# Two chunks of a triangular inversion run five steps ahead of the other two, and a masking step is issued one step later

## What is computed

```
m = where(strict, einsum(k_beta, k) * decay, 0)
t_inv = triangular_solve(eye + m, eye)
u = t_inv @ (v * beta);  w = t_inv @ (k_beta * exp(g))
for each chunk:                                   # the scan
    v_new = u_i - w_i @ state
    o = (q_i * exp(g_i)) @ state + a_i @ v_new
    state = state * exp(g_last) + k_dec^T @ v_new
```

## Time and profile before

| what | us |
|---|---|
| median of 3 runs | 1057.03 (1056.55 to 1057.26) |
| the profiled execution, its own time | 1057.9 |
| its span in the trace | 1056.1 |
| stretch from the last projection to the first x step | 186.64 to 235.66 |
| stretch of the levels, x7 and t | 235.66 to 349.72 |
| from there to the scan's second kb product | 349.72 to 364.26 |

### The profile page before, as it was taken

How to read it: one execution, slowest core, us unless ns; L and a number is a source line. 1 busy time by engine, 2 the same in 40 slices (tenths; PEclk the granted TensorE clock), 3 DMA queues, 4 the chain that set the end, 5 groups by cost and what they waited for, 6 DMA issues and landing times.

```text
span 1056.1 us, 12807 instructions
## 1 busy us (share of the span) xinstructions
PE 972.5 (92%) x5186; PEld 820.8 (78%) x5186; DVE 499.6 (47%) x812; ACT 470.4 (45%) x821; POOL 450.8 (43%) x253
## 2 busy tenths in 40 slices
PE   6999798759999899999998979899999999999987
PEld 5987576649999797777776758788888888888876
DVE  5057764487675345324246432433333333564434
ACT  6464566435654144334376541453333433332223
POOL 4528344570002363143577642245354443454440
PEclk9999999869999899999999999999999999999998
DMA  9423110000001007133322222133323232333302
GB/s 352 133 77 98 62 41 1 1 1 1 2 27 55 1 22 259 52 120 100 89 72 61 64 86 71 47 114 100 100 83 117 80 107 93 100 100 100 100 20 80
DMA packets 25162, 84.07 MB, mean 80 GB/s; under 512 B 2992, under 2 KB 3248, under 8 KB 24976
## 3 DMA queue, kind: packets, MB, share of 16 engines
q1 hardware_dynamic: 24240, 82.14, 23.9%
q10 hardware_dynamic: 864, 1.12, 0.3%
HBM read 79.06 MB, written 2.10 MB: 77 GB/s over the span
## 4 chain that ended last, share of the span: by engine, by line
PE 74%; DVE 12%; ACT 8%; POOL 3%; issue 2%; DMA 0%; SPq 0%; DVEq 0%; ACTq 0%
PE bank L1889 72%; DVE qk L1439 2%; PE bank L1897 2%; ACT wh L1111 1%; ACT L1111 1%; POOL wl L1005 1%; DVE xl L1433 1%; DVE dd L1433 1%; DVE vc L1439 1%; ACT sl L1111 1%; DVE mp L1433 1%; ACT ee L1111 1%; ACT xs L1111 1%; ACT qk L1111 1%; DVE xf L1433 1%
## 5 line engine op out<-in xcount | busy, mean ns | idle before, releaser
L1005 POOL TENSOR_TENSOR wl<-raw,wh 128x1024 fp32r<-128x1024 f32 (+1 forms) x131 | 316.6, 2421 | 389.8 <-ACT wh L1111 389.7
L1889 PE MATMUL bank<-xh,wh 128*128 128x512 f32 (+1 forms) x536 | 207.8, 388 | 6.8 <-DVE xl L1433 4.8
L1889 PE MATMUL bank<-xh,wl 128*128 128x512 f32 (+1 forms) x536 | 205.9, 384 | 0.0
L1889 PE MATMUL bank<-xl,wh 128*128 128x512 f32 (+1 forms) x536 | 205.9, 384 | 0.0
L1111 ACT ACTIVATE wh<-raw 128x1024 fp32r<-128x1024 f32 (+1 forms) x131 | 135.7, 1042 | 133.5 <-PE bank L1889 127.3
L1889 PE MATMUL bank<-wh,xh 128*128 128x512 f32 (+1 forms) x352 | 140.1, 398 | 18.1 <-POOL wl L1005 10.4
L1889 PE MATMUL bank<-wh,xl 128*128 128x512 f32 (+1 forms) x352 | 135.0, 384 | 0.0
L1889 PE MATMUL bank<-wl,xh 128*128 128x512 f32 (+1 forms) x352 | 134.8, 383 | 0.0
L1889 PEld LDWEIGHTS bank<-xh,wh 128*128 128x128 f32 x536 | 101.5, 189 | 28.2 <-issue 6.0
L1889 PEld LDWEIGHTS bank<-xh,wl 128*128 128x128 f32 x536 | 101.4, 189 | 19.8
L1889 PEld LDWEIGHTS bank<-xl,wh 128*128 128x128 f32 x536 | 101.5, 189 | 19.0
(11 more groups left out here) (249 smaller groups left out, 1566.4 us busy)
## 6 DMA issues: line engine op xcount, KB each, us to landing
raw<-in_wflat SPq DMA_DIRECT2D x127, 512.0 KB, 3.4
xt<-in_xt SPq DMA_DIRECT2D x8, 256.0 KB, 4.3
h<-in_x SPq DMA_DIRECT2D x4, 512.0 KB, 6.8
h<-in_x SPq DMA_DIRECT2D x1, 2048.0 KB, 9.7
gain<-in_pr SPq DMA_DIRECT2D x3, 512.0 KB, 3.4
consts<-in_cf SPq DMA_DIRECT2D x1, 1472.0 KB, 10.8
raw<-in_wflat SPq DMA_DIRECT2D x4, 272.0 KB, 10.9
kh<-kh SPq DMA_DIRECT2D x8, 128.0 KB, 2.3
```

The costliest lines, as they stand in the source:

```text
L1005: e.tensor_tensor(WL[u % NS][:, 0:n], RAW[u % NS][:, 0:n], WH[u % NS][:, 0:n].bitcast(F32), ALU.subtract).then_inc(w_lo.up(u), 1)
L1889: return e.matmul(o, l, r_, start=start, stop=stop, skip_group_check=part)
```

## The change

Three things change.
- DVE's masking of mp into dd and ACT's copy of mp into mr leave the step m. They become a step of their own, inv_dd, which stands at the head of the next step of the same chunk, ahead of mt.
- The order: chunks 0 and 3 are taken through decay, kq, m and mt first, with seven steps of attention between. Then come 14 rounds: one step of chunk 0, two of attention, one of chunk 3, two of attention, and then one step of chunk 1, one of attention, one of chunk 2, one of attention. Chunks 1 and 2 begin these rounds with their decay, so they are five steps behind. After the 14 rounds, chunks 0 and 3 are done and chunks 1 and 2 have five steps left (d at level 5, x and d at level 6, x7, t).
- The first vb of the scan waits for the inverse of chunks 0 and 3.

```diff
--- before.py
+++ after.py
@@ -515,6 +515,7 @@
         BI.let_go(("inv", cb, "k"))
         do("inv_m", cb)
         yield
+        do("inv_dd", cb)
         for d in range(2):
             take(("mt", d), (inv_v, ("dt", cb, 0, d)))
         do("inv_mt", cb)
@@ -600,19 +601,25 @@
             step(gi[0])
     while step(g1):
         pass
-    step(gi[1], 2)
     BI.over((0, 1, 2, 3, 4))
     gs = swa()
     for b in (5, 6, 7):
         BANK[("swa", b)] = (b, emptied[b])
-    for g in gi[2:]:
-        step(g, 2)
+    for cb, n in ((0, 1), (3, 2), (0, 1), (3, 1), (0, 1), (3, 1), (3, 1)):
+        step(gi[(0, 3, 1, 2).index(cb)], n)
+        step(gs)
+    ahead = 14
     live = True
-    while live:
+    while ahead or live:
         live = False
-        for g in gi:
+        for g in gi[:2]:
+            if ahead:
+                step(g)
+                step(gs, 2)
+        ahead -= ahead > 0
+        for g in gi[2:]:
             live = step(g) or live
-            step(gs, 2)
+            step(gs, 1 if ahead else 2)
     do("z_gain")
     while step(gs):
         pass
@@ -1060,7 +1067,7 @@
             W = SCAN[d]
             if r == 0:
                 on.wait_ge(*inv_v.at(("t", 0, 1)))
-                on.wait_ge(*inv_v.at(("t", 2, 1)))
+                on.wait_ge(*inv_v.at(("t", 3, 1)))
                 on.wait_ge(*swa_g.at(3))
             else:
                 on.wait_ge(*scan_p.at(("av", d, r - 1)))
@@ -1256,7 +1263,7 @@
             on.wait_ge(*inv_a.at(("ee1", cb, d)))
             act(ee, ee, ACT.Exp, inv_a.up(("ee", cb, d)), scale=-1.0)
 
-        def inv_m(cb):
+        def inv_mr(cb):
             for d in range(2):
                 on.wait_ge(*inv_g.at(("m", cb, d)))
                 act(WORK[cb]["MR"][d][:], MP[cb][:, d, :], ACT.Copy, inv_a.up(("mr", cb, d)))
@@ -1418,7 +1425,7 @@
             e.dma_start(ov[:, tb, 0:512], OUT[:, tb, 0:512]).then_inc(s_out[0], 16)
 
         return dict(begin=begin, x_split=x_split, rms_row=rms_row, prep=prep, stat=stat, split=split, conv=conv, square=square, qsum=qsum, qexp=qexp, to_tok=to_tok,
-                    gate1=gate1, gate2=gate2, rope_root=rope_root, rope_t=rope_t, tok=tok, inv_decay=inv_decay, inv_m=inv_m,
+                    gate1=gate1, gate2=gate2, rope_root=rope_root, rope_t=rope_t, tok=tok, inv_decay=inv_decay, inv_dd=inv_mr,
                     inv_d=inv_d, swa_s=swa_s, swa_t=swa_t, swa_o=swa_o, scan_keys=scan_keys, scan_v=scan_vn, scan_o=scan_o,
                     dn_sq=dn_sq, forget=forget, cum_a=cum_a, gelu=gelu, qk2=qk2, fa_exp=fa_exp, fa_t=fa_t, fa_o=fa_o_, fa_split=fa_split,
                     gm_root=gm_root, up_post=up_post,
@@ -1601,6 +1608,9 @@
             for d in range(2):
                 on.wait_ge(*inv_g.at(("mb", cb, d)))
                 tt(MP[cb][:, d, :], psum[b][:, :], W["MB"][d][:], ALU.mult, inv_v.up(("m0", cb, d)))
+
+        def inv_dd(cb):
+            W = WORK[cb]
             for d in range(2):
                 on.wait_ge(*inv_g.at(("m", cb, d)))
                 tt(h3(W["DD"][d][:]), h3(MP[cb][:, d, :]), bc4(cf("LM", 7 * (1 - d))), ALU.mult, inv_v.up(("dd", cb, 0, d)))
@@ -1874,7 +1884,7 @@
                 stt(OUT[:, tb, c], H[:, tb, c], rr, GAIN[:, c], ALU.mult, ALU.mult, fin_v.up(("out", tb, n)))
 
         return dict(begin=begin, x_split=x_split, conv_rms=conv_rms, scale=scale, split=split, masks=masks, conv=conv, qexp=qexp, gate1=gate1, gate2=gate2, rope_sq=rope_sq,
-                    rope_root=rope_root, rope_scale=rope_scale, rope=rope, rope_t=rope_t, inv_decay=inv_decay, inv_kq=inv_kq, inv_m=inv_m,
+                    rope_root=rope_root, rope_scale=rope_scale, rope=rope, rope_t=rope_t, inv_decay=inv_decay, inv_kq=inv_kq, inv_m=inv_m, inv_dd=inv_dd,
                     inv_mt=inv_mt, inv_x=inv_x, inv_d=inv_d, inv_x7=inv_x7, inv_t=inv_t, swa_s=swa_s, swa_t=swa_t, swa_o=swa_o,
                     scan_o=scan_o, dn_mul=dn_mul, tok=tok, resid=resid_, fa_const=fa_const, forget=forget, cum_b=cum_b, qk2=qk2, fa_s=fa_s,
                     fa_norm=fa_norm, fa_t=fa_t, fa_o=fa_o_, fa_split=fa_split, gm_sum=gm_sum, gm_rec=gm_rec, gm_norm=gm_norm, gm=gm, up_post=up_post, a_prep=a_prep,
```

## The result

The changed kernel is slower: 1100.07 us (median of 4 runs, 1094.29 to 1100.66) against 1057.14 of the kernel before. The ratio is 1.0381, with a 95% interval of 1.0357 to 1.0404. The forecast was 1047.0, with a range of 1041 to 1055.

A forecast was written before the change was run, and what follows sets the result against it. PE issue bounds the levels; 35 us are lost in the masking stretch and handover, with DVE the next bound. Gains 5.9 - 1.5 + 5.6 = 10.0 us take 1057.9 to 1047.9 profiled, 1047.0 median; range 1041.0 to 1055.0.

The forecast's parts named there:

- The stretch of levels: Rounds behind the masking (x and d steps): PE's work unchanged and still the bound, 1.7 us lost before.
- Rival D: Masking stretch: clock stays low as PE is thinly fed, 362 instructions take 82.5 us, kernel ends at 1067.0; chance 0.07.
- Edit 1: dd and mr one step later: DVE's four direct waits for POOL go (3.1 us), dd kept at 1.34 us.
- rival C: Masking stretch: dd no longer meets POOL, costs 0.68 instead of 1.34, 5.3 us off; time 1041.7; chance 0.15.
- Edit 2's first stretch: Chunks 0 and 3 ahead, until all masking is done: DVE-bound, 62.5 us, 21.2 lost against 27.1, gain 5.9 us.
- The tail of two chunks: Inversion's end with chunks 1 and 2: they do not quite cover the last division, loss 1.5 us (0 to 3).
- Edit 3: Handover to the scan: first vb waits for chunks 0 and 3; 8.9 us where 14.5 stood, gain 5.6 us.
- Rival B: Handover gains nothing: attention's end, z_gain and vb come too late, PE waits for vb; time 1052.6; chance 0.10.
- Rival A: Masking stretch gains nothing: DVE idle 14.4 us again, chain through POOL is the bound; time 1052.9; chance 0.12.
- The sum: Whole kernel: 5.9 - 1.5 + 5.6 = 10.0 us gained, profiled execution 1047.9, median 1047.0 us.

The follow-up runs named there:

- Experiment 1: Changed kernel plus 12 PE filler products of 512 columns before chunk 0's d step at level 3; 1047.47 us, ratio 0.9886.
- experiment 6: Changed kernel plus wide PE fillers before chunk 0's d steps at level 2 (10) and level 3 (12); 1048.20 us, ratio 0.9902.
- experiment 9: Changed kernel plus 24 narrow PE fillers of 128 columns before chunk 0's d step at level 3; 1048.30 us, ratio 0.9894.
- experiment 5: Kernel before plus six extra DVE multiplies ahead of chunk 0's xf at level 2, to make PE wait; 1125.98 us, ratio 1.0625.
- experiment 4: Kernel before, old order and old scan wait, with only dd and mr moved one step later; 1136.63 us, ratio 1.0726.
- experiment 2: Changed kernel plus 12 wide PE fillers before chunk 0's d step at level 5; median 1078.66 us, profiled run 1059.4.
- experiment 3: Changed kernel with dd and mr put back in the step m, so without their delay; 1057.59 us, ratio 0.9989.
- experiment 10: Kernel before with dd one step later, plus 16 wide PE fillers before chunk 0's d step at level 1; 1064.64 us, ratio 1.0061.
- experiment 12: Changed kernel plus 24 narrow PE fillers of 128 columns before chunk 0's d step at level 5; 1103.49 us, ratio 1.0433.
- experiment 7: Changed kernel plus 12 wide PE fillers at chunk 0's level 3 and 14 before mt of chunks 0 and 3; 1052.11 us, ratio 0.9946.

## Why the prediction was wrong, point by point

**The stretch of levels** is the step that failed. The prediction wrote: "The work of PE is the same and stays the bound", and gave it a loss of 1.7 us for small waits and 1.5 for the division. It priced a wait of PE by its own length. Two waits of 2.4 us together stand where the clock fell, and 51.4 us more go by behind them, because every instruction costs 0.213 us instead of 0.114 until chunk 0's x7. Experiments 1, 6, 9 and 5 show it from both sides: with products in the place of the first wait the new order takes 1047.5 to 1048.3, and the old order with such waits takes 1126.0. What in the work behind a wait lifts the clock, and what leaves it down, stays open.

**Rival D** had the right mechanism, a clock that stays low, and was given 0.07. Its place and its size were wrong. It was put into the thin rounds up to round 5, where the clock was at 0.50 from 200 to 215 us and then came back (0.86 over the first of the windows above), and was bounded by that stretch's 362 instructions. I took the dense stretch to be safe because in the earlier trace rows it ran at 1.00. But those rows show only that it keeps the clock it comes with, not that it would take it back.

**Edit 1** was read as harmless. The prediction let DVE's direct waits (3.1 us) go and kept dd at 1.34 us. In the new order 2.5 us of the waits stay, 1.74 for chunk 0 and 0.78 for chunk 3: with one step of attention between, POOL's addition isn't done. Only the old order loses them (0.0 in experiment 4). The prediction did not ask what stands around the new place: dt behind, the attention maximum behind that, and POOL's at masks beside. dd came to 1.48 us in the new order and 1.56 in the old one, rival C's 0.68 is what the shortest takes and no mean is near it, and by itself the edit costs 78 us (experiment 4).

**Edit 2's first stretch** had the right bound, and DVE's work came out: 51.9 us against 51.5. The rest did not: the sum put 11 us on it (9 of idle DVE, 2 of slow clock), and DVE was idle for 13.8. The stretch took 65.7 us against 62.5. At 0.114 each its 373 instructions are worth 42.5 us, and PE was busy for 50.9, so that slow clock cost PE 8.4 us there. What the sum had as 21.2 us of loss was 23.2, and the gain 3.9 us instead of 5.9. A stretch that DVE bounds has PE waits somewhere; the prediction summed them and did not say where each would fall. Where they fall decided the case.

**The tail of two chunks** was right in kind and too dear: PE waited 0.40 us for the xf behind the last division, where the sum has a loss of 1.5:

```profile
385.25 1.17 PE L1899 MATMUL bank<-xf,dd 128*128 128x128 f32 x8 [0.40 <-DVE xf L1440]
```

**Edit 3** was right: 9.15 us against 8.9, by the bank and not by vb. Rival B is out. Rival A is out by its time but not by its sign: DVE was idle for 13.8 us, near its 14.4. Its price was wrong: by the prediction's own terms 51.5 and 14.4 make 65.9 us, nearly what was measured, and that is a gain of 2.5 us and not of nothing.

**The sum** of all but the clock came out, and in part by luck. Experiment 1's profiled execution took 1047.3 us, and the forecast for one was 1047.9. But its first stretch took 65.7 us and not 62.5. The work behind it up to PE's last t took 92.3, where the sum has 96.2 (816 instructions at 0.114, 1.7 and 1.5). The two errors cancel. The gain of the change, with a filler in it, is some 10 us, and the clock's price about five times that.

On the clock the Trainium skill (TensorE: Matmul & The Clock Gate, Part 1) says that the throttled state is the default and that activity releases it. For the first half the traces show only that the clock is at 0.50 behind waits. The second does not cover these traces: PE was busy for 110.8 of 110.8 us in the changed kernel, 140 of 140 in experiment 5 and 189.3 of 190 in experiment 4, and the clock was not released. Here the measurement decides.

## What to carry to other kernels

Where long runs of small products follow a place at which PE may wait, price the wait by the clock behind it and not by its length, and look in the trace for what last raised the clock and whether it still comes after the new wait. A step moved behind another one is to be looked at with its new neighbours on its own queue and on GpSimd's, not only freed of its old wait. If a schedule that should win comes out slower at a low granted clock, a few spare products in the wait are a cheap test, and here they were also the better kernel (1047.5 us against 1058.1).

## What was not expected of the hardware

- PE was busy for 189.3 of 190 us and stayed at 1.2 GHz (experiment 4). Between 186 us and the end of the inversion the clock came back in or right behind kq products (202 us before), in the products of the decay steps (216 us in the changed kernel), in mt transposes (230 us before, about 258 us in experiments 2 and 3), in x7 steps (363 us in the changed kernel, about 406 us in experiment 5), and once within a block of wide products (247 us in experiment 10). In no trace did it come back within a run of x and d steps with attention pieces alone. Why those and not these was not settled: 24 narrow products lifted nothing (experiment 12), while three runs with 12 wide ones at the same place took some 21 us less than the changed kernel, without a trace that shows why.
- The same program can take 20 us more or less from one run to the next: 1059.4 and 1078.2 to 1079.9 us (experiment 2), 1064 and 1097 us (experiment 10). The mean granted clock differs with them (0.966 and 0.952 in the one, 0.972 to 0.976 and 0.939 in the other). Where it fell in the runs without a trace was not seen.
- With the clock kept up where PE had been idle, it fell later, at 215 us, where PE had work (experiment 7, 1052.1 us against 1047.5).
